# Recurrence gates of a hybrid decoder layer: three products of rounded high and low parts in place of one fp32 product, and the low parts of the third weight block on VectorE

## The reference, cut to what matters

```
xa = causal_depthwise_conv(z[..., :1024], conv_w, conv_b)          # four taps
xh = xa.reshape(b, s, 16, 64)                                      # 16 heads of 64
r = sigmoid(einsum('bshi,hij->bshj', xh, w_r) + b_r)
i = sigmoid(einsum('bshi,hij->bshj', xh, w_i) + b_i)
log_a = -8 * r * softplus(-lam);  a = exp(log_a)
u = sqrt(-expm1(2 * log_a)) * (i * xa)
h = associative_scan(h[t] = a[t] * h[t-1] + u[t])
ha = h * gelu(ya)
```

## Time and profile before

| | us |
|---|---|
| device time, median of 3 runs | 892.82 (889.98 to 893.69) |
| device time of the profiled execution | 892.09 |
| its span, first to last instruction | 890.3 |
| PE busy in the span | 841.5 (95%) |
| DVE busy | 335.3 (38%) |
| ACT busy | 266.3 (30%) |
| POOL busy | 90.2 (10%) |

### The profile page before, as it was taken

How to read it: one execution, slowest core, us unless ns; L and a number is a source line. 1 busy time by engine, 2 the same in 40 slices (tenths; PEclk the granted TensorE clock), 3 DMA queues, 4 the chain that set the end, 5 groups by cost and what they waited for, 6 DMA issues and landing times.

```text
span 890.3 us, 10283 instructions
## 1 busy us (share of the span) xinstructions
PE 841.5 (95%) x4265; PEld 527.1 (59%) x4265; DVE 335.3 (38%) x467; ACT 266.3 (30%) x388; POOL 90.2 (10%) x63
## 2 busy tenths in 40 slices
PE   5999999999999999899999999888998897999996
PEld 4778877788888888536535344352352352633675
DVE  6699539952762616511020120101100102013964
ACT  7565336633242326202010100101001001003767
POOL 3429580000000000000000000000000000000000
PEclk9999999999999999999999999999899999999999
DMA  9222222211524762999999999999999999998902
GB/s 260 94 93 95 94 95 95 95 47 48 189 95 188 301 266 105 385 428 426 403 425 430 427 428 427 428 429 428 424 428 428 427 426 429 428 422 323 350 1 95
DMA packets 44758, 253.85 MB, mean 285 GB/s; under 512 B 8804, under 2 KB 9896, under 8 KB 31912
## 3 DMA queue, kind: packets, MB, share of 16 engines
q1 hardware_dynamic: 42120, 248.21, 68.9%
q0 software_dynamic: 2304, 4.20, 1.2%
q10 hardware_dynamic: 288, 0.79, 0.2%
HBM read 246.89 MB, written 10.49 MB: 289 GB/s over the span
## 4 chain that ended last, share of the span: by engine, by line
PE 76%; DMA 15%; DVE 5%; issue 2%; ACT 2%; POOL 0%; DVEq 0%; POOLq 0%; ACTq 0%
PE bank L1364 75%; DMA ring<-in_w_down_e_dram 11%; DMA ring<-in_w_up_e_dram 3%; DVE r L1297 1%; DVE r L1292 1%; PE bank L1571 1%; DMA r<-in_x_dram 1%; DVE ring_rounded L399 1%; DVE r_rounded L1008 0%; DVE r_rounded L399 0%; PE bank L1426 0%; ACT L973 0%; ACT junk L706 0%; DVE ring_rounded L1008 0%; ACT r_rounded L715 0%
## 5 line engine op out<-in xcount | busy, mean ns | idle before, releaser
L1364 PE MATMUL bank<-ring_rounded,ring_rounded 128*128 128x512 f32 (+1 forms) x680 | 239.4, 389 | 1.3 <-DVE r_rounded L1008 1.3
L1364 PE MATMUL bank<-r_rounded,ring_rounded 128*128 128x512 f32 (+1 forms) x744 | 237.8, 393 | 0.8 <-DVE ring_rounded L1008 0.8
L1364 PEld LDWEIGHTS bank<-r_rounded,ring_rounded 128*128 128x128 f32 x744 | 138.9, 188 | 32.4 <-issue 2.4
L1364 PEld LDWEIGHTS bank<-ring_rounded,ring_rounded 128*128 128x128 f32 x680 | 127.5, 188 | 29.9 <-issue 2.4
L1364 PE MATMUL bank<-ring,gain 128*64 128x512 f32 x472 | 118.0, 604 | 9.6 <-issue 5.0
L1364 PE MATMUL bank<-ring,hT 128*64 128x512 f32 x400 | 112.3, 624 | 6.6 <-DMA ring<-in_w_down_e_dram 6.6
L1364 PE MATMUL bank<-ring,junk 128*64 128x512 f32 x472 | 115.4, 592 | 0.0
L683 POOL DMA_INDIRECT expert_rows<-r,row_i x16 | 15.6, 977 | 674.0 <-DVE r L1258 398.4
L1364 PEld LDWEIGHTS bank<-ring,gain 128*64 128x64 f32 x472 | 35.8, 138 | 76.9 <-issue 69.0
L1364 PEld LDWEIGHTS bank<-ring,junk 128*64 128x64 f32 x472 | 37.2, 137 | 71.9 <-issue 71.8
L1364 PEld LDWEIGHTS bank<-pick,r_rounded 128*128 128x128 f32 x576 | 72.6, 199 | 9.9 <-issue 8.5
(11 more groups left out here) (212 smaller groups left out, 765.5 us busy)
## 6 DMA issues: line engine op xcount, KB each, us to landing
ring<-in_w_up_e_dram SPq DMA_DIRECT2D x31, 2048.0 KB, 29.1
ring<-in_w_gate_e_dram SPq DMA_DIRECT2D x25, 2048.0 KB, 27.4
ring<-in_w_down_e_dram SPq DMA_DIRECT2D x22, 2048.0 KB, 32.0
ring<-in_w_in_dram SPq DMA_DIRECT2D x18, 1024.0 KB, 7.4
r<-in_w_down_e_dram SPq DMA_DIRECT2D x5, 2048.0 KB, 33.1
r<-in_w_gate_e_dram SPq DMA_DIRECT2D x5, 2048.0 KB, 27.8
ring<-in_w_down_e_dram SPq DMA_DIRECT2D x7, 1024.0 KB, 21.4
r<-in_x_dram SPq DMA_DIRECT2D x8, 512.0 KB, 8.1
```

The lines of the kernel that those rows point to most:

```text
L1364: return nc.tensor.matmul(*a, **k)
```

## The change

The gates' operands get high and low parts too, and each of the two fp32 products becomes three fp32r products. For the weights, ACT makes `diag_high` (128 by 2048) once `lru_in` is complete, ahead of `split_high` of half (1, 0), and POOL subtracts `diag_low` in place, between the low parts of block 0 and those of block 1. For the data, ACT makes `xc_high(c)` at the start of its work for the tile after the convolution's, ahead of the `split_high` there; DVE makes `xc_low(c)`: behind `conv` for c = 0, 1, 4 and 5, and inside `lru(c - 2)`, behind the reciprocal, for c = 2, 3, 6 and 7. PE waits for `xc_low_ready` where it waited for `conv_done`. The low parts of block 2 go from POOL to DVE, at tile 5, ahead of `lru(3)`.

```diff
-    low_engine = {(n, h): "pool" if n < FIRST_MERGE and n != 3 and (n, h) != (0, 1) else "vector" for n, h in halves}
+    low_engine = {(n, h): "pool" if n < FIRST_MERGE and n not in (2, 3) and (n, h) != (0, 1) else "vector" for n, h in halves}
...
+        diag_high = slot_r[7][:, 0:NX * 2 * P].rearrange("p (c w j) -> p c w j", c=NX, w=2)
+        diag_low = r3_r[:, 0:NX * 2 * P].rearrange("p (c w j) -> p c w j", c=NX, w=2)
...
             low(0)
+            pool.wait_ge(diag_high_ready, 1)
+            nc.gpsimd.tensor_tensor(diag_low, diag, diag_high, ALU.subtract).then_inc(diag_low_ready, 1)
             low(1)
-            low(2)
...
             nc.scalar.activation(spt[:, 1, :], spt[:, 0, :], ACT.Exp, scale=-1.0).then_inc(decay_exp, 1)
+            act.wait_ge(lru_in, 16 * 11)
+            nc.scalar.activation(diag_high, diag, ACT.Copy).then_inc(diag_high_ready, 1)
             split_high(act, 1, 0)
...
+            def xc_split(c):
+                act.wait_ge(conv_done, c + 1)
+                if c >= 2:
+                    act.wait_ge(gates_psum, c - 1)
+                nc.scalar.activation(xc_high(c), xc[:, c % 4, :], ACT.Copy).then_inc(xc_high_ready, 1)
...
             for t, (kind, c) in enumerate(tiles):
                 n = t // 4
+                if t >= 1 and tiles[t - 1][0] == "xa":
+                    xc_split(tiles[t - 1][1])
                 if t >= 1 and (n + 1, t % 4) in halves:
                     split_high(act, n + 1, t % 4)
...
+            def xc_split(c):
+                dve.wait_ge(xc_high_ready, c + 1)
+                if c >= 2:
+                    dve.wait_ge(gates_psum, c - 1)
+                v.tensor_tensor(xc_low(c), xc[:, c % 4, :], xc_high(c), ALU.subtract).then_inc(xc_low_ready, 1)
+
-            def lru(c):
+            def lru(c, meanwhile=None):
...
                 after(v.reciprocal(q, q))
+                if meanwhile is not None:
+                    xc_split(meanwhile)
...
                 if t >= LAG and tiles[t - LAG][0] == "xa":
-                    lru(tiles[t - LAG][1])
+                    lru(tiles[t - LAG][1], c if kind == "xa" else None)
+                elif kind == "xa":
+                    xc_split(c)
...
             def lru_gates(c):
-                pe.wait_ge(conv_done, c + 1)
+                pe.wait_ge(xc_low_ready, c + 1)
...
-                    pe.wait_ge(lru_in, 16 * 11)
+                    pe.wait_ge(diag_low_ready, 1)
                 for w in range(2):
-                    ins = mm(bank[4 + 2 * (c % 2) + w][:, :], diag[:, c, w, :], xc[:, c % 4, :], start=True, stop=True)
+                    dst = bank[4 + 2 * (c % 2) + w][:, :]
+                    mm(dst, diag_high[:, c, w, :], xc_high(c), start=True, stop=False)
+                    mm(dst, diag_low[:, c, w, :], xc_high(c), start=False, stop=False)
+                    ins = mm(dst, diag_high[:, c, w, :], xc_low(c), start=False, stop=True)
```

More of the change, by code:

```diff
@@ L136, in build, with xc_high, xc_low @@
         gel = scr[:, 10 * S:12 * S].rearrange("p (b t) -> p b t", b=2)
+        diag_high = slot_r[7][:, 0:NX * 2 * P].rearrange("p (c w j) -> p c w j", c=NX, w=2)
+        diag_low = r3_r[:, 0:NX * 2 * P].rearrange("p (c w j) -> p c w j", c=NX, w=2)
+        def xc_high(c):
+            return slot_r[7][:, 6 * S:7 * S] if c % 2 == 0 else slot_r[5][:, 0:S]
+        def xc_low(c):
+            return slot_r[7][:, 7 * S:8 * S] if c % 2 == 0 else slot_r[5][:, S:2 * S]
         xbp = r4[:, :].rearrange("p (g t) -> p g t", g=NB)
@@ L278, in build @@
         conv_done = sem("conv_done")
+        diag_high_ready = sem("diag_high_ready")
+        diag_low_ready = sem("diag_low_ready")
+        xc_high_ready = sem("xc_high_ready")
+        xc_low_ready = sem("xc_low_ready")
         gates_psum = sem("gates_psum")
```

## The result

| | us |
|---|---|
| before, median of 4 runs | 892.88 (889.98 to 893.69) |
| after, median of 4 runs | 898.63 (897.73 to 901.04) |
| ratio, with its 95% interval | 1.0075 (1.0044 to 1.0105) |
| profiled execution of after | 901.04 (span 899.3) |
| forecast, and its range | 898.0, 889.5 to 901.5 |

The changed kernel is slower by 5.8 us, for which the forecast said 5.9 over the profiled execution. The median hit the forecast almost to the point. But one term of the sum did not happen as written and others were missing from it, and that these cancel is partly luck. The profiled execution of after is its slowest, with a span of 899.3, 9.0 us over the profiled one of before; the others had spans of 896.0 to 897.5. So the last 3 us of its lag cannot be put down to the change.

A forecast was written before the change was run, and what follows sets the result against it. The prediction took PE's stream through the dense blocks to bound the kernel. Saving and three waits summed to -3.2 + 3.5 + 3.4 + 2.2 = +5.9 us, so 892.1 + 5.9 = 898.0; range 889.5 to 901.5.

The forecast's parts named there:

- The bound: PE's stream through all dense blocks sets the end; a shift before 329 us carries to the end in full.
- Part 1: PE at the gates: six rounded products replace two fp32 ones, saving 0.40 us for each c, 3.2 us in all.
- Part 2: At the start, two POOL subtractions hold DVE's tiny decay chain, so the first convolution starts at 35.4, not 28.58.
- Part 3: Gates 0: the operand is ready at 39.1, PE is there at 35.65 and waits 3.5 us.
- Part 4: Gates 1 to 3: xc_low(3) is ready at 62.9, PE needs it at 59.5 and waits 3.4 us.
- rival (c): PE's clock halves after idle stretches; behind the wait at tile 8 this costs up to 3.3 us, 901.3; chance 0.08.
- Part 5: Tile 8: block 2's low parts on DVE come late behind lru(2) and POOL's windows; PE waits 2.2 us.
- Part 6: Gates 4 to 7 and the rest: no wait of PE, with a margin of 1 us.

The follow-up runs named there:

- PE kept busy: The changed kernel with 26 transposes of the identity into a free bank on PE ahead of its wait at gates 0; 897.91 us.
- the edit of the table: Run alone: the kernel before with only the low parts of block 2 moved to DVE; 891.32 us, ratio 0.9997.
- the chain first: The changed kernel with POOL's diag_low subtraction waiting until DVE's decay chain is over; 893.33 us.
- through PSUM: The changed kernel with the running sum of DVE's decay chain in a PSUM bank in place of SBUF; 893.40 us.

## Why the prediction was right, and where it was not

- **The bound.** PE's stream through the dense blocks was to set the end, and its shift there to carry to the end. Right as far as the dense end: 7.3 us there, 5.8 where the experts begin. That the shift carries to the end in full is not shown: the router stage took 1.5 from it in this pair, and in the expert stage, where the chain passes through the loads, it was anything from 4.8 to 10.0.
- **Part 1, the saving.** 0.40 us for each gate, right: rounds of 6.81 us for 7.20, and 1.6 us for four gates in the kernel with gates 4 to 7 only.
- **Part 2, the hold.** Right, and it is the finding: two holds, convolution 0 at 34.96 (35.4 reckoned). What the rows had not shown, that the tiny two-input operation is held, is shown by 9.83 us with its operands in SBUF and 1.22 with one in PSUM. That one DVE operation and one of POOL's in a queue take turns was assumed, and held too. That "a DVE operation between SBUF tensors waits out a POOL subtraction" was too wide: the `RECIPROCAL` of line 1068 did not.
- **Part 3, first wait.** 3.5 reckoned, 3.0 measured; the chain was over 0.4 us earlier than reckoned.
- **Part 4, second wait.** `xc_low(3)` was reckoned for 62.9 and came at 62.33. PE was not there at 59.5 to wait, because the clock had fallen. This is the step that failed, though not the sum. The prediction had the fall of the clock, and that this wait would take it up, in its rival (c). It should have stood in the forecast, and the second term been written as wait or clock, whichever is longer: 3.4 reckoned as a wait, 3.0 of clock and 0.3 of wait measured. With PE kept busy the wait was 3.03.
- **Part 5, third wait.** 2.2 reckoned, 2.0 measured, in part by luck: of the 2.6 us put on for POOL's windows, the subtraction itself got nothing (2.26 against 2.28), while the steps of `lru` ahead of it, from 62.33 to 76.38, took 14.1 us for 11.4. That the old place would have had the low parts in time was wrong for a kernel whose start is late: they would have been there at 79.92, not at 71.14, and the gelu would have waited besides. The term belongs to the lateness of the start, not to the edit of the table, which alone costs nothing.
- **Part 6.** No wait at gates 4 to 7, right. The small wait of 0.2 at 229.6 was in no term.
- **Rival (c)** came true in small: behind the third wait the clock fell for 3.4 us and cost 1.7, which the sum had not. The router stage gave back 1.5 in that execution. That these two cancel is why the experts begin 5.8 us late, close to the 5.9 of the sum. That the median fell on the forecast as well is luck as far as these runs tell: the profiled execution itself was 3.0 over it.

What stays open: why the clock fell at the wait of 1.96 us in after and not at those of the same length in the kernels with the chain first and through PSUM; how often the router's second gather is the one at the lower clock; and what moves the lag by 5 us in the expert stage.

## What to carry over

Before giving POOL a long operation on SBUF, look at what DVE does in that time. It is not the size of DVE's operations that counts: one that takes 0.17 us alone took 4.5 beside POOL, and a dependent chain met such a hold twice, once for each POOL operation in line. A saving on the engine that bounds the kernel is worth its full price only where its operands' producer has room, so spread such an edit by stages: the half of this one that lies where DVE has room gained 1.4 us, and the whole lost 5.8. And where a wait follows whose end another engine sets, a fall of the clock ahead of it costs nothing as long as it eats no more than that wait; only what lies behind the last one counts.

## What the runs showed of the hardware

- Six dependent `SCALAR_TENSOR_TENSOR` of 128 by 8 elements took 9.83 us beside two POOL subtractions of 4.6 us in a row, 1.17 us without, and 1.22 us beside them with one operand in PSUM. Two of the six took that time, 4.48 and 4.52 us; the first of them ended at 29.51, where the first subtraction gave way to the second (29.48).
- A `TENSOR_SCALAR` with one SBUF input (128 by 16 elements) was held too, 3.80 us for 0.17 (line 1067 of the kernel with the chain through PSUM). A `RECIPROCAL` of the same shape with one SBUF input was not: 0.25 us beside POOL's next subtraction.
- The granted clock fell to its lower level 2 us into a stand of 3.0 us in after and stayed there for 6.8 us. Each time it went in one step, within a stretch of 1 us. Two other stands of 3.0 us, at gates 0 with block 2 back on POOL and at gates 3 with PE kept busy, were followed by 3.4 us at the lower level, which began 0.4 and 1.2 us behind the end of the stand. Of three stands of 1.96 us (at tile 8 in after, with the chain first and through PSUM) one was followed by 3.4 us and two by none. So the length of a stand did not tell the cost in these runs: 3.0, 1.7 and 1.7 us behind stands of 3.0, and 1.7, 0 and 0 behind stands of 1.96.
